# Inverse of the first delta rule on 32x32 diagonal blocks, with its running value kept in PSUM

## The chip, the core and the metric

The kernel runs on one core of a Trainium2 chip. The core has a matrix engine (TensorE, here PE, its weight loads PEld), three engines for elementwise work (VectorE or DVE, ScalarE or ACT, GpSimd or POOL), a queue that starts DMA transfers (SyncE, SP), an on-chip memory of 128 partitions, and PSUM, eight banks of 512 f32 per partition that PE writes. The engines run their own instruction lists and wait for each other with semaphores. The metric is device time in microseconds of one execution, median of several.

## The reference, cut to what matters

Two transformer layers over 256 tokens of width 2048. The second layer has two recurrences side by side. The first (16 heads of 64, "rwkv7") is

```
Sa = einsum('bhvk,bhk->bhv', S, a_t)
S  = S * w_t + Sa * b_t + v_t * k_t ;  y_t = S r_t
```

The kernel does it by chunks of 64 tokens: 4 chunks x 16 heads = 64 pairs. For each pair it needs the inverse of a unit triangular 64x64 matrix I - N, with N made of products of a and b of the chunk. Two pairs lie above each other in the 128 partitions (chunk c in partitions 64c to 64c+63), so a tile "of 32 units" [128, 32, 64] holds all of them; unit 16 cp + x is head x of chunk pair cp. The second recurrence (gated delta rule, 8 heads of 128) has its own inverse, which stands behind the first recurrence and is not changed. It needs decay matrices exp(F_i - F_j), masked to one triangle, for 8 heads and two halves of the tokens (tiles gd_x and gd_aqk_t).

## The kernel before, in words

Most of the kernel streams weights through PE in three products each (high and low parts). The change lies in the stretch between the input projection of the second layer and its output projection, where PE runs small f32 products. Every engine's list is written out by hand; an engine takes its instructions in that order, and a wait holds all that stand behind it.

**The inverse.** The products that fill N and the three other triangles (`gram_products`, groups i of the list GRAMS, banks from GRAM_BANKS) go through DVE (`gram_masks`), which multiplies by masks, writes nt_r, akt, rbt and rkt, and puts the 1x1 level under the diagonal of x_r and of xt_r with predicated copies. Then five levels k = 0 to 4 double the size of the inverted blocks. A level has, for each quarter b of the units (8 units), `inverse_z` (PE: N times X, 64x64 products), a mask of level k+1 on DVE into z_r, `inverse_x` (PE: X transposed times Z), an addition into x_r on DVE, and `inverse_turn`, the transpose of x_r into xt_r on DVE. The last level writes xt_r alone. Quarters of one level are interleaved on PE and DVE. Between them stand `value_products` (z1, copied by ACT), `decay_rows` (PE spreads the sums of the second recurrence's gates to PSUM, from which ACT makes both decay tiles with Relu and Exp) and the key grams of the second recurrence (L1227).

**Behind it.** Four groups make wt (L1239, copied by ACT at L1796) and the inverted values in banks 4 to 7 (L1164 again). On DVE `gd_lower` (L2600) multiplies the key grams into gd_x and `gd_begin` (L2641, L2643) cuts out its chunks.

**The recurrence.** Four turns g: PE multiplies the state into the values (L1255), DVE and ACT copy a half each into rw_u (L2657, L1802), PE makes the state products (L1270, L1276, L1283) and outputs (L1290, L1291), DVE updates the state (L2667, L2668). In turns 2 and 3 PE also transposes gd_x (L1265). DVE multiplies the sigmoid of z into proj2 in turn 1 (L2660), ACT makes this sigmoid in turn 0 (L1804). The query products (L1324) follow, then the second inverse.

POOL masks the decay tiles with affine_select (L643) and makes the first state (L637). SP starts the first two weight loads of the output projection when the recurrence's outputs are made.

Of the kernel before, what the change touches and what calls it, by code (L numbers as in the profile page):

```python
# [12 lines left out]
ALU = mybir.AluOpType  # L13
# [3 lines left out]
P = 128  # L17
# [52 lines left out]
def build(nc, a, out):  # L70
    ctx = ExitStack()
    with ctx:
# [171 lines left out]
        x_r = slot("rw_x", HO + 8 * KB, UNITS)  # L244
        GRAMS = [(cp, kind, g) for cp in range(2) for kind, g in (("b", 0), ("b", 1), ("x", 0), ("k", 0), ("k", 1))]
        GRAM_BANKS = (0, 2, 4, 6, 0, 2, 4, 6, 2, 6)
        xt_r, z_r = slot("rw_xt", R0, UNITS), slot("rw_z", R1, UNITS)
# [3 lines left out]
        gn_sq = slot("gn_squares", R5)  # L251
# [18 lines left out]
        z_sig = slot("gd_z_sig", R1)  # L270
# [12 lines left out]
        def bcc(m, n):  # L283
            return m.unsqueeze(1).to_broadcast([P, n, 64])


# [7 lines left out]
                "e_prev", "kk_root", "e_plus", "e_minus", "gd_sig_qk", "gd_sq", "gd_l2_root", "gd_sig_v", "gate_kept", "at_kept"],  # L294
            "vector": ["wf_spread", "f_raw", "rnn_out", "rows_rounded", "x_rescaled", "lora_lo", "ab_out", "lora_out", "lora_in", "kk", "r_shifted", "gd_cum",
                "gd_tok_out", "l_prev", "gd_scalars", "kk_mean", "kk_rows", "rk", "kk_out", "at_made", "rw_bonus", "gd_cv_qk", "rt_made",
                "gd_silu_qk", "bt_made", "gd_cv_v", "gd_l2_mean", "kw_made", "gd_silu_v", "l2_rows", "gd_qk"],
# [142 lines left out]
        def _(sp):  # L440
# [106 lines left out]
        def _(gp):  # L547
# [85 lines left out]
            for x in (x_r, xt_r):  # L633
                last = gp.tensor_copy(x[:], bcc(chunk_eye, 32))
            last.then_inc(step("eyes_made"), 1)
            gp.wait_ge(S("rw_gram"), 20)
            gp.memset(state[:], 0.0).then_inc(S("rw_state"), 1)  # L637
            for half in range(2):
                hs = slice(4 * half, 4 * half + 4)
                for o, g, base, cm in ((0, x_g, -1, 1), (1, aqk, 0, -1)):  # L640
                    v = g[:].rearrange("p (c h) n -> p c h n", c=2)[:, :, hs, :]
                    gp.wait_ge(S("gd_gam"), 2 * half + o + 1)
# [15 lines left out]
        def _(pe):  # L658
# [477 lines left out]
            def gram_products(i):  # L1136
# [6 lines left out]
                l = {"b": bt_f, "k": Kw, "x": None}[kind]  # L1143
                for n in range(4 * g, 4 * g + 4) if l is not None else range(8):
                    for c in range(2):
                        tc = slice((2 * cp + c) * CH, (2 * cp + c + 1) * CH)
                        for half in range(2):
                            r = slice(64 * half, 64 * half + 64)
                            o = bank(GRAM_BANKS[i] + half)[64 * c:64 * c + 64, :]
                            if l is None:  # L1150
                                last = mm(o[:, n * 64:(n + 1) * 64], at_f[r, n, tc], bt_f[r, n, tc], start=(n == 0), stop=True,
                                          skip_group_check=True)
                            else:
                                last = mm(o[:, (n % 4) * P:(n % 4 + 1) * P].rearrange("p (m t) -> p m t", m=2), l[r, n, tc],
                                          AR[r, :, n, tc], start=(n % 4 == 0), stop=True, skip_group_check=True)
# [12 lines left out]
            def value_products(cp):  # L1168
                if cp:
                    pe.wait_ge(S("rw_z1_out"), 1)  # L1170
                pe.wait_ge(S("rw_gram_out"), 20)
                for b in range(2):
                    last = of_chunks(bank(2 + b), lambda r, u: akt[r, u, :], lambda r, u: v_tok2[r, u // 16, hc(u % 16)], 8,
# [3 lines left out]
            def inverse_z(k, b):  # L1177
                pe.wait_ge(S("inv_x_out"), 4 * k + b + 1)
                wait(pe, S("inv_z_out"), 4 * k + b - 1)
                of_chunks(bank(b % 2), lambda r, u: nt_r[r, u, :], lambda r, u: x_r[r, u, :], 8, 8 * b).then_inc(S("inv_z"), 1)  # L1180

            def inverse_x(k, b):
                pe.wait_ge(S("inv_z_out"), 4 * k + b + 1)
                if k == 0:
                    pe.wait_ge(S("rw_gram_out"), 20 if b >= 2 else 14)
                else:
                    pe.wait_ge(S("inv_xt_out"), 4 * k - 4 + b + 1)
                x_lhs, x_rhs = (xt_r, z_r) if k < 4 else (z_r, xt_r)
                of_chunks(bank(4 + b), lambda r, u: x_lhs[r, u, :], lambda r, u: x_rhs[r, u, :], 8, 8 * b).then_inc(S("inv_x"), 1)

            def decay_rows(half):
                pe.wait_ge(S("gd_fall"), 2 * half)
                over_heads(2, row_sums[:], 4 * half, 4 * half + 4,
                           sel_r[0:2 * H, :].bitcast(F32)).then_inc(step(f"gd_g_rows{half}"), 1)

            for i in range(8):
                gram_products(i)
            for k in range(5):
                if k == 0:
                    pe.wait_ge(S("rw_gram_out"), 10)  # L1200
                inverse_z(k, 0)
                if k == 0:
                    gram_products(8)
                inverse_z(k, 1)
                if k == 0:
                    gram_products(9)
                inverse_x(k, 0)
                inverse_z(k, 2)
                inverse_x(k, 1)
                if k == 0:  # L1210
                    value_products(0)
# [1610 lines left out]
```

## Time and profile before

| | us |
|---|---|
| device time, median of 3 runs | 2889.12 (2886.62 to 2892.81) |
| span of the profiled execution | 2882.8 |
| PE busy in it | 2851.3 (99%) |
| DVE busy | 1590.1 (55%) |
| ACT busy | 1164.0 (40%) |
| POOL busy | 70.5 (2%) |

The span is from the first to the last instruction of the profiled execution; the device time is measured around the whole launch. In the view of 40 slices each digit is a tenth. A record is one instruction as the profiler saw it: each f32 product of the small stages leaves two weight loads and two matmuls. In the lists of time, a row merges neighbouring records of one kind: the first number is the start, the second the time from the first start to the last end, xN their count. "128*128" or "64*64" is rows times columns of the array that a matmul uses.

### The profile page before, as it was taken

To read this page: it belongs to the slowest core of one execution; us is meant where nothing else is said; L and a number is where in the kernel's file an instruction comes from. 1 tells how busy PE (TensorE), PEld (TensorE's weight loads), DVE (VectorE), ACT (ScalarE), POOL (GpSimd) and SP (SyncE) were. 2 spreads that over 40 slices of the span, in tenths; PEclk is the share of its full clock that TensorE was granted. 3 is DMA by queue.
4 is the path that set the end of the run, shared out by engine and by line. 5 is a ranking of instruction groups with operands and counts; after the bars stand their busy time and mean duration, and the time that the engine had idled before them with its cause. 6 is when DMAs were issued, how large, how long until landed. Compare 5 with 4: busy or idle time off the path is not lost.

```text
span 2882.8 us, 41255 instructions
## 1 busy us (share of the span) xinstructions
PE 2851.3 (99%) x17984; PEld 2456.9 (85%) x17984; DVE 1590.1 (55%) x1321; ACT 1164.0 (40%) x952; POOL 70.5 (2%) x130
## 2 busy tenths in 40 slices
PE   8999999999999999999999999999999999999998
PEld 8999888888888888888889999998788888888887
DVE  5757554544555554454447667876664545454445
ACT  4345443333443333333335443433444333333333
POOL 0000000000000000002002000010000000000000
PEclk9999999999999999999999999999999999999999
DMA  6555556666555555555556544400355555555554
GB/s 223 165 162 186 163 161 190 190 194 192 184 189 190 189 189 189 189 189 190 191 195 220 171 136 159 149 3 33 111 181 190 189 190 189 189 189 189 190 194 170
DMA packets 257441, 501.09 MB, mean 174 GB/s; under 512 B 12288, under 2 KB 17739, under 8 KB 256923
## 3 DMA queue, kind: packets, MB, share of 16 engines
q1 hardware_dynamic: 257307, 499.06, 53.4%
q8 instruction: 113, 1.85, 0.3%
q14 instruction: 21, 0.17, 0.0%
HBM read 496.74 MB, written 2.10 MB: 173 GB/s over the span
## 4 chain that ended last, share of the span: by engine, by line
PE 96%; DVE 3%; ACT 0%; issue 0%; DMA 0%; SPq 0%; DVEq 0%; ACTq 0%
PE psum L724 23%; PE psum L726 23%; PE psum L725 23%; PE psum L709 5%; PE psum L712 5%; PE psum L711 5%; PE psum L1164 2%; DVE weight_lo L1934 1%; PE psum L775 1%; PE psum L1039 0%; PE psum L663 0%; PE psum L1024 0%; PE psum L890 0%; PE psum L910 0%; PE psum L900 0%; DVE rw_gram L2566 0%
## 5 line engine op out<-in xcount | busy, mean ns | idle before, releaser
L1934 DVE TENSOR_TENSOR weight_lo<-weight_raw,weight_hi 128x2048 fp32r<-128x2048 f32 x460 | 1054.2, 2292 | 1088.7 <-ACT weight_hi L1470 1088.1
L1470 ACT ACTIVATE weight_hi<-weight_raw 128x2048 fp32r<-128x2048 f32 x460 | 881.6, 1916 | 1495.8 <-PE psum L726 1210.0
L724 PE MATMUL psum<-weight_hi,h_both 128*128 128x512 f32 x1856 | 724.9, 391 | 0.0
L726 PE MATMUL psum<-weight_hi,h_both 128*128 128x512 f32 x1856 | 722.5, 389 | 0.0
L725 PE MATMUL psum<-weight_lo,h_both 128*128 128x512 f32 x1856 | 722.1, 389 | 0.0
L726 PEld LDWEIGHTS psum<-weight_hi,h_both 128*128 128x128 f32 x1856 | 348.4, 188 | 72.8
L725 PEld LDWEIGHTS psum<-weight_lo,h_both 128*128 128x128 f32 x1856 | 348.6, 188 | 71.3
L724 PEld LDWEIGHTS psum<-weight_hi,h_both 128*128 128x128 f32 x1856 | 348.5, 188 | 71.3
L709 PE MATMUL psum<-h_both,weight_hi 128*128 128x256 f32 x1408 | 401.6, 285 | 6.8 <-DVE weight_lo L1934 6.7
L711 PE MATMUL psum<-h_both,weight_lo 128*128 128x256 f32 x1408 | 398.4, 283 | 0.0
L712 PE MATMUL psum<-h_both,weight_hi 128*128 128x256 f32 x1408 | 398.3, 283 | 0.0
L709 PEld LDWEIGHTS psum<-h_both,weight_hi 128*128 128x128 f32 x1408 | 270.0, 192 | 11.7 <-DVE weight_lo L1934 5.8
L711 PEld LDWEIGHTS psum<-h_both,weight_lo 128*128 128x128 f32 x1408 | 270.1, 192 | 0.1
L712 PEld LDWEIGHTS psum<-h_both,weight_hi 128*128 128x128 f32 x1408 | 270.1, 192 | 0.0
L724 PE MATMUL psum<-weight_hi,ffn_hi 128*128 128x512 f32 x672 | 261.9, 390 | 0.0
L726 PE MATMUL psum<-weight_hi,ffn_lo 128*128 128x512 f32 x672 | 261.5, 389 | 0.0
L725 PE MATMUL psum<-weight_lo,ffn_hi 128*128 128x512 f32 x672 | 261.4, 389 | 0.0
L724 PEld LDWEIGHTS psum<-weight_hi,ffn_hi 128*128 128x128 f32 x672 | 126.1, 188 | 26.5 <-issue 0.6
L726 PEld LDWEIGHTS psum<-weight_hi,ffn_lo 128*128 128x128 f32 x672 | 126.1, 188 | 26.2
L725 PEld LDWEIGHTS psum<-weight_lo,ffn_hi 128*128 128x128 f32 x672 | 126.1, 188 | 26.1
L726 PE MATMUL psum<-weight_hi,y_lo 128*128 128x512 f32 x320 | 125.2, 391 | 0.0
L724 PE MATMUL psum<-weight_hi,mixed_hi 128*128 128x512 f32 x256 | 101.5, 396 | 3.3 <-DVE y_lo L2771 3.3
(526 smaller groups left out, 2184.1 us busy)
## 6 DMA issues: line engine op xcount, KB each, us to landing
weight_raw<-in_w_in SPq DMA_DIRECT2D x144, 1024.0 KB, 5.4
weight_raw<-in_w_ffn_in SPq DMA_DIRECT2D x88, 1024.0 KB, 5.0
weight_raw<-in_w_ffn_out SPq DMA_DIRECT2D x44, 1024.0 KB, 5.1
weight_raw<-in_ffn_w_gate SPq DMA_DIRECT2D x44, 1024.0 KB, 5.1
weight_raw<-in_ffn_w_up SPq DMA_DIRECT2D x44, 1024.0 KB, 5.2
weight_raw<-in_ffn_w_down SPq DMA_DIRECT2D x44, 1024.0 KB, 5.1
weight_raw<-in_w_out SPq DMA_DIRECT2D x32, 1024.0 KB, 5.2
weight_raw<-in_w_branch_rnn SPq DMA_DIRECT2D x8, 1024.0 KB, 5.1
```

Of the source, the lines that this page charges most:

```text
L709: mm(acc[:, f, :], wh[:, k, c], xh, start=(start and k == 0 and f % 2 == 0), stop=False, skip_group_check=True)
L711: mm(acc[:, f, :], wl[:, k, c], xh, start=False, stop=False, skip_group_check=True)
L712: last = mm(acc[:, f, :], wh[:, k, c], xl, start=False, stop=(stop and k == CK - 1), skip_group_check=True)
L724: mm(acc[:, t, :], xh[:, c], wh[:, k, :], start=(start and k == 0), stop=False, skip_group_check=True)
L725: mm(acc[:, t, :], xh[:, c], wl[:, k, :], start=False, stop=False, skip_group_check=True)
L726: last = mm(acc[:, t, :], xl[:, c], wh[:, k, :], start=False, stop=(stop and k == CK - 1), skip_group_check=True)
L775: last = tr(pair(2)[:, k, t * P:(t + 1) * P], act_up[:, t, k * P:(k + 1) * P], ident[:])
L1164: last = mm(o[r, u * 64:(u + 1) * 64], lhs(r, u0 + u), rhs(r, u0 + u), start=(u == 0), stop=True, skip_group_check=True)
L1470: A(hi[j % g.hi][:], raw[j % g.ring][:], ACT.Copy).then_inc(hi_ready, 1)
L1934: V.tensor_tensor(lo[r][:], raw[r][:], hi[j % g.hi][:].bitcast(F32), ALU.subtract).then_inc(lo_ready, 1)
```

## The change

The inverse now works on the two 32x32 blocks on the diagonal of each 64x64 matrix. They are kept in compact tiles of 32 columns (x_c, xt_c, z_c: [128, 32, 32]), four blocks above each other in the partitions. Levels k = 0 to 3 run on halves cp of 16 units, and each product is a 32x32 one at partitions 32q (`block_products`). The value of X is kept in PSUM (bank cp): an identity product puts the first X there (`inverse_begin`), each level's product adds to it, and ACT copies it to x_c (`block_copy`), from where DVE turns it. The last level, the lower corner of each 64x64 matrix, is two products of 32x32 blocks (`corner_z`, `corner_x`, with an identity product in front of the second) and copies into the two column halves of xt_r. The gram groups come in another order with other banks; the x grams are only made for the diagonal blocks; the predicated copies into xt_r are gone.

The decay differences are made by two engines: ACT makes gd_x with Relu (`decay_falls`), DVE makes gd_aqk_t with subtract and min (`decay_rises`), each starting at another bank. The four Exp come at the end, and the masks of gd_x before those of gd_aqk_t. DVE copies wt in place of ACT (`key_states`). The inverted values of the second chunk pair move into turn 2 of the recurrence; gd_lower and gd_begin move into turns 0 and 1, the silu of z to the end of turn 2, its sigmoid to turn 2. POOL builds masks of 32 columns (block_masks, upper_rows). SP's second weight load waits for gn_var too, since gn_squares and rw_z now share memory with its ring slot.

The core of the diff:

```diff
+        x_c, xt_c, z_c = slot("rw_x", HO + 8 * KB, BLOCKS), slot("rw_xt_blocks", HO + 12 * KB, BLOCKS), slot("rw_z", R1, BLOCKS)
...
+        GRAMS = [(cp, kind, g) for cp in range(2) for kind, g in (("b", 0), ("b", 1), ("x", 0))] + \
+                [(cp, "k", g) for cp in range(2) for g in range(2)]
+        GRAM_BANKS = (0, 2, 4, 6, 4, 6, 4, 6, 4, 6)
...
             for j, src in enumerate(wo2.sources(0)):
+                if j == 1:
+                    sp.wait_ge(*at_step("gn_var"))
...
+            def block_products(b, lhs, rhs, cp, start):
+                for u in range(16 * cp, 16 * cp + 16):
+                    for q in range(4):
+                        r = slice(32 * q, 32 * q + 32)
+                        last = mm(bank(b)[r, (u % 16) * 32:(u % 16 + 1) * 32], lhs(r, u, q % 2), rhs(r, u), start=(start and u % 16 == 0),
+                                  stop=True, skip_group_check=True)
+                return last
+            def inverse_begin(cp):
+                pe.wait_ge(S("rw_gram_out"), 6 + 6 * cp)
+                pe.wait_ge(*at_step(f"turned{cp}"))
+                mm(bank(cp), ident[:], x_c[:, quarter(cp), :].rearrange("p u n -> p (u n)"), start=True, stop=False,
+                   skip_group_check=True)
+            def inverse_z(k, cp):
+                if k:
+                    pe.wait_ge(*at_step(f"x_out{k - 1}{cp}"))
+                block_products(2 + cp, lambda r, u, b: nt_r[r, u, 32 * b:32 * b + 32], lambda r, u: x_c[r, u, :], cp,
+                               True).then_inc(step(f"inv_z{k}{cp}"), 1)
+            def inverse_x(k, cp):
+                pe.wait_ge(*at_step(f"z_out{k}{cp}"))
+                pe.wait_ge(*at_step(f"turned{k - 1 if k else ''}{cp}"))
+                block_products(cp, lambda r, u, b: xt_c[r, u, :], lambda r, u: z_c[r, u, :], cp, False).then_inc(step(f"inv_x{k}{cp}"), 1)
+            def corner_z(cp):
+                pe.wait_ge(*at_step(f"x_out3{cp}"))
+                for u in range(16 * cp, 16 * cp + 16):
+                    for c in range(2):
+                        r = slice(64 * c, 64 * c + 32)
+                        last = mm(bank(2 + cp)[64 * c + 32:64 * c + 64, (u % 16) * 32:(u % 16 + 1) * 32], nt_r[r, u, 32:64], x_c[r, u, :],
+                                  start=(u % 16 == 0), stop=True, skip_group_check=True)
+                last.then_inc(step(f"inv_z4{cp}"), 1)
+            def corner_x(cp):
+                pe.wait_ge(*at_step(f"turned3{cp}"))
+                pe.wait_ge(*at_step(f"z_out4{cp}"))
+                mm(bank(2 + cp), ident[:], xt_c[:, quarter(cp), :].rearrange("p u n -> p (u n)"), start=True, stop=True,
+                   skip_group_check=True)
...
+            for i in range(4):
+                gram_products(i)
+            inverse_begin(0)
+            inverse_z(0, 0)
+            gram_products(4)
+            inverse_x(0, 0)
+            gram_products(5)
+            inverse_z(1, 0)
+            gram_products(6)
+            inverse_begin(1)
+            inverse_z(0, 1)
+            inverse_x(1, 0)
+            gram_products(7)
...
+            inverse_z(3, 0)
+            value_products(0)
+            inverse_z(2, 1)
+            inverse_x(3, 0)
+            value_products(1)
+            inverse_x(2, 1)
+            corner_z(0)
+            decay_rows(0)
+            inverse_z(3, 1)
+            corner_x(0)
+            inverse_x(3, 1)
+            corner_z(1)
+            decay_rows(1)
+            corner_x(1)
+            key_states(0)
+            inverted_values(0)
+            key_states(1)
+            key_products()
...
+                if g == 2:
+                    inverted_values(1)
+                    pe.wait_ge(S("rw_uv"), 2)
...
+            def block_copy(k, cp):
+                act.wait_ge(*at_step(f"inv_x{k}{cp}"))
+                A(x_c[:, quarter(cp), :], blocks_of(cp), ACT.Copy).then_inc(step(f"x_out{k}{cp}"), 1)
...
+            def inverse_turn(k, cp):
+                dve.wait_ge(*at_step(f"x_out{k}{cp}"))
+                V.transpose(xt_c[:, quarter(cp), :], x_c[:, quarter(cp), :]).then_inc(step(f"turned{k}{cp}"), 1)
...
+            def decay_rises(half):
+                dve.wait_ge(*at_step(f"gd_g_rows{half}"))
+                for b in (1, 0):
+                    if b == 0:
+                        dve.wait_ge(S("gd_fall"), 2 * half + 1)
...
+                if g == 2:
+                    dve.wait_ge(S("gd_z_sig"), 1)
+                    V.tensor_tensor(proj2[:, 40:48, :], proj2[:, 40:48, :], z_sig[:], ALU.mult).then_inc(S("gd_z_silu"), 1)
+                if g < 2:
+                    gd_lower(g, 0, 8)
+                    dve.wait_ge(S("gd_n"), g + 1)
+                    gd_begin(x_gc, x_g, low_c[0], g).then_inc(S("gd_x_out"), 1)
```

## Rows read from the trace of the kernel before

**Rows 1.** The page: span, busy time of PE, granted clock by 40 slices.

```profile
span 2882.8 us, 41255 instructions
PE 2851.3 (99%) x17984; PEld 2456.9 (85%) x17984; DVE 1590.1 (55%) x1321; ACT 1164.0 (40%) x952; POOL 70.5 (2%) x130
...
PEclk9999999999999999999999999999999999999999
```

**Rows 2.** Windows of the stage: us, busy time (records) of five engines, clock, DMA.

```profile
1894.45:1903.28 8.83, 8.29 (x322) 7.19 (x321) 7.33 (x15) 1.02 (x1) 0.00 (x0) 1.00 0.03 6
1903.28:1955.50 52.22, 50.16 (x1503) 48.50 (x1504) 41.41 (x72) 15.73 (x39) 4.80 (x5) 1.00 0.01 3
1955.50:1963.79 8.29, 7.82 (x267) 7.42 (x263) 8.16 (x21) 2.17 (x4) 0.00 (x0) 1.00 0.02 6
1963.79:1987.42 23.63, 23.47 (x721) 22.72 (x721) 10.81 (x14) 10.98 (x16) 0.00 (x0) 1.00 0.01 3
```

**Rows 3.** Chain that ended last, pieces in the inverse: start, us, what.

```profile
1909.63 14.14 PE psum L1164 x480
1923.77 1.92 PE psum L1045 x8
...
1935.37 10.66 PE psum L1164 x352
...
1957.24 0.60 DVE rw_xt L2586
```

**Rows 4.** Waits, 1894.5 to 1987.4: total us, times, longest.

```profile
DVE rw_z L2579 <- PE psum L1164: 10.2, 8, 2.4
```

**Rows 5.** List by time, PE, small products: start, us, line, tile, operands, count.

```profile
1957.88 2.08 PE L1164 MATMUL psum<-rw_z,rw_xt 64*64 64x64 f32 x64 [0.42 <-DVE rw_xt L2586]
...
1896.25 1.11 PE L1151 MATMUL psum<-proj,a_tilde_r 64*64 64x64 f32 x64
...
1896.25 0.24 PE L1151 MATMUL psum<-proj,a_tilde_r 64*64 64x64 f32 x4
...
1718.37 0.36 PE L1063 MATMUL psum<-ident,gdn_b 16*128 16x8 f32 x2
1718.60 0.36 PE L1064 MATMUL psum<-ident,gdn_small 16*128 16x8 f32 x2
```

**Rows 6.** The same list: one-tile products and what follows them.

```profile
1945.96 2.05 PE L1227 MATMUL psum<-proj 128*128 128x128 f32 x16
1947.94 0.27 PE L1164 MATMUL psum<-rw_x,rw_gram 64*64 64x64 f32 x2
...
1991.41 3.64 PE L1039 MATMUL psum<-gn_squares,head_cols 128*32 128x256 f32 x16
1994.98 0.33 PE L1164 MATMUL psum<-gd_z_chunks,gd_xt_chunks 64*64 64x64 f32 x4
```

**Rows 7.** Groups by line, 1883 to 2037: busy us, mean ns, idle before, releaser.

```profile
L2579 DVE TENSOR_TENSOR rw_z<-psum,chunk_masks 128x512 f32<-128x512 f32 x20 | 13.6, 680 | 10.4 <-PE psum L1164 10.2 <-DVE rw_x L2551 0.3
...
L1812 ACT ACTIVATE gn_squares<-psum 128x512 f32<-128x512 f32 x4 | 2.4, 592 | 0.0
```

**Rows 8.** List by time, DVE: gd_lower and gd_begin before the recurrence.

```profile
1957.74 2.16 DVE L2600 SCALAR_TENSOR_TENSOR gd_x<-psum,gdn_token_scalars,gd_x 128x128 f32<-128x128 f32 x8
...
1959.93 1.39 DVE L2641 TENSOR_TENSOR gd_x_chunks<-gd_x,chunk_masks 64x512 f32<-64x512 f32 x2
...
1961.35 0.69 DVE L2643 TENSOR_TENSOR gd_x_chunks<-gd_x_chunks,chunk_masks 128x512 f32<-128x512 f32 x1
```

**Rows 9.** DMA queue of instructions and busy time, 1890 to 1990.

```profile
q8 instruction: 23, 0.38, 1.7%
...
1890.00:1990.00 100.00, 96.76 (x2878) 92.62 (x2877) 70.65 (x122) 32.95 (x64) 8.78 (x8) 1.00 0.03 7
```

**Rows 10.** Windows around the one fall of the clock near the stage.

```profile
2068.50:2074.01 5.51, 2.25 (x13) 1.57 (x13) 4.91 (x5) 4.03 (x3) 0.00 (x0) 1.00 0.58 182
2074.00:2080.00 6.00, 5.99 (x19) 4.80 (x20) 3.29 (x2) 0.00 (x0) 0.00 (x0) 0.72 0.02 9
```

More of the change, by code:

```diff
@@ new lines, in corner_x @@
+            def corner_x(cp):
[3 more added lines that the diff above has]
+                   skip_group_check=True)
+                for u in range(16 * cp, 16 * cp + 16):
+                    for c in range(2):
+                        r = slice(64 * c + 32, 64 * c + 64)
+                        last = mm(bank(2 + cp)[64 * c:64 * c + 32, (u % 16) * 32:(u % 16 + 1) * 32], z_c[r, u, :], xt_c[r, u, :],
+                                  start=(u % 16 == 0), stop=True, skip_group_check=True)
+                last.then_inc(step(f"inv_x4{cp}"), 1)
@@ new lines, in decay_rows, with key_products @@
+            def decay_rows(half):
+                if half:
+                    pe.wait_ge(S("gd_fall"), 2)
+                    pe.wait_ge(S("gd_rise"), 2)
+                else:
+                    pe.wait_ge(S("rw_z1_out"), 1)
+                over_heads(4, row_sums[:], 4 * half, 4 * half + 4,
+                           sel_r[0:2 * H, :].bitcast(F32)).then_inc(step(f"gd_g_rows{half}"), 1)
+            def key_products():
+                pe.wait_ge(S("gd_fall"), 4)
+                pe.wait_ge(S("gd_rise"), 4)
+                for c in range(2):
+                    tk = slice(c * P, (c + 1) * P)
+                    for h in range(4):
+                        last = mm(bank(4 + c)[:, h * P:(h + 1) * P], cv[:, 4 + h, tk], cv[:, 4 + h, tk], start=(h == 0), stop=True,
+                                  skip_group_check=True)
+                last.then_inc(step("gd_gram"), 1)
@@ L1236, in _, with key_states @@
+            def key_states(cp):
+                pe.wait_ge(*at_step(f"xt_left{cp}"))
+                pe.wait_ge(*at_step(f"xt_right{cp}"))
+                if cp == 0:
+                    pe.wait_ge(*at_step("x_out31"))
+                    pe.wait_ge(*at_step("turned31"))
+                for n in range(8):
+                    for half in range(2):
                         for c in range(2):
-                            x = 8 * (b % 2) + n
+                            x = 8 * half + n
                             tp = slice(64 * c, 64 * c + 64)
@@ L1260, in _ @@
                 if g >= 2:
+                    pe.wait_ge(S("gd_n"), g - 1)
                     if g == 3:
@@ new lines, in _ @@
+            for k, cp in ((0, 0), (1, 0), (0, 1), (2, 0), (1, 1)):
+                block_copy(k, cp)
+            values_copy(0)
+            block_copy(3, 0)
+            values_copy(1)
+            block_copy(2, 1)
+            decay_falls(0)
+            block_copy(3, 1)
+            decay_falls(1)
+            for o, g in ((0, x_g), (1, aqk)):
+                for half in range(2):
+                    act.wait_ge(S("gd_rise" if o else "gd_fall"), 2 * half + 2)
+                    v = g[:].rearrange("p (c h) n -> p c h n", c=2)[:, :, 4 * half:4 * half + 4, :]
+                    A(v, v, ACT.Exp, scale=1.0 if o else -1.0).then_inc(S("gd_gam"), 1)
@@ L1838, in _ @@
             scaled_k(1)
-            act.wait_ge(*at_step("gn_var"))
+            act.wait_ge(S("gd_z_silu"), 1)
             chunk_hi(1)
@@ L2593, in gd_lower, with key_states @@
+            def key_states(cp):
+                dve.wait_ge(S("rw_wt"), cp + 1)
+                for g in (2 * cp, 2 * cp + 1):
+                    last = V.tensor_copy(wt[:, :, g * CH:(g + 1) * CH], bank(g).rearrange("p (n t) -> p n t", n=NT))
+                last.then_inc(S("rw_wt_out"), 1)
             def gd_lower(c, h0, h1):
@@ L2648, in chunk_turn @@
                 V.transpose(xt_gc[:, u, :], x_gc[:, u, :]).then_inc(S("gd_xt_out"), 1)
-            dve.wait_ge(S("gd_n"), 2)
-            for b in range(2):
-                gd_begin(x_gc, x_g, low_c[0], b).then_inc(S("gd_x_out"), 1)
             for g in range(4):
```

289 lines of the change are left out of this document (126 added, 163 removed), and 2 rows, old and new, of the table STEPS.

## The prediction

> **What bounds the kernel now.** The page comes first: PE is busy 99% of the span and its clock is full in nearly every slice [rows 1]. But the change touches one stage only, so I cut the span at that stage with the windows view. From 1894.45 us (first gram product) to 1987.42 us (query products, the first work that the change leaves alone) are 92.97 us; PE is busy 89.7 of them, DVE 67.7, ACT 29.9 [rows 2]. The reader should see that DVE is nearly full only in the first window (7.33 of 8.83) and in the third (8.16 of 8.29), and PE in all four. The chain of waits says the same: long unbroken pieces of the 64x64 products at L1164, between them the spread rows at L1045, while DVE enters it only before 1909 and around 1955 [rows 3]. The view of waits has DVE waiting 10.2 us for L1164 [rows 4]. So in the inverse PE's instruction stream sets the end, and what changes there goes to the total one for one: nothing behind it hangs on absolute time, because each later weight load is released by steps of this chain.
>
> **The unit of price.** Each f32 product leaves two records on PE. 64 records of 64x64 tiles last 2.08 us from first start to last end, one record 0.22, so 63 gaps share 1.86 us: 29.5 ns a record where two tiles of the array take turns [rows 5]. The x-gram products use four tiles: (1.11-0.22)/63 = 14.1 ns [rows 5]. Both are some 58 ns for one tile. 256 columns on one tile take 3.57/16 = 223 ns a record [rows 6], and loading 128 weight columns against 8 moving ones takes 112 ns (two records each 0.225 us) [rows 5]. So a tile costs about 0.87 ns for each column, moving or weight, whichever is more, and a 32x32 product keeps its tile for about 30 ns. The new products walk over four diagonal tiles: 30/4 = 7.5 ns. Four x-gram records start inside 0.24-0.22 = 0.02 us, 7 ns apart [rows 5]; that is the closest that PE is seen to issue in a run of four. I take 8 ns. The trace has nothing that lasts at such a rate: 14.1 ns is the fastest over 64 records. Ends: 6.5 ns and 14.1 ns.
>
> **The change part by part (PE).** A. Removed: twenty z and twenty x groups of 32 records, 29.2 ns each in my sum (the 29.5 above holds small waits), 40 x 0.93 = 37.4 us. B. Added: 4 levels x 2 halves x 2 = 16 block products of 128 records, 16 x 1.02 = 16.4 us. C. Corner products, 4 groups of 64 records on only two tiles, 30/2 = 16 ns: 4.1 us (2.0 at 8 ns, 7.5 at 29.2). D. Four identity products of 512 columns, two records each, 2 x 0.446 from L1039 [rows 6]: 3.6 us. E. x grams: 256 records of 8 ns for 128 of 14.6: +0.2. F. key_states alternates halves and so uses four tiles where L1239 used two: 128 records at 14.6 for 29.2, -1.9. Grams, value products, decay rows, key grams and inverted values keep number and price; inverted_values(1) only moves to the third turn of the recurrence, where PE is serial too. Sum: 37.4 - 16.4 - 4.1 - 3.6 - 0.2 + 1.9 = 15.0 us less work.
>
> G. Changes of tile shape. The 16 turns L1227 start at 1945.96 and the next product at 1947.94 [rows 6]: 1.98 us for 16 x 0.112 = 1.79, so about 0.17 us for coming back. Before, the stage has 10 changes of shape; afterwards I count 35 in the written order (32x32, 64x32, 64x64, 128x128, and 16 rows). 25 x 0.17 = +4.3 us. Whether 64x64 to 32x32 costs what 128x128 to 64x64 does no row shows: ends 0.05 and 0.4, that is +1.3 and +10.
>
> H. Waits. 92.97 less work at these prices (85.0) less ten changes (1.7) leaves 6.3 us of waiting before. For afterwards I walked the new orders of PE, DVE and ACT with 0.69 us for each 128x512 step on DVE and 0.59 on ACT [rows 7] and 0.2 behind the last product. A level of one half costs 1.2 + 0.7 + 1.2 + 0.6 = 3.7 us, and the four products of a level with their grams need over 4 us of PE, so the two halves hide each other. Four holes remain: 1.2 us before the first product (PE waits for masks and the turn of half 0), 0.9 at the second corner, and two of 2.0 us in the recurrence. Those come from moved DVE work: gd_lower and gd_begin now stand behind the state update of turns 0 and 1. Eight steps at L2600 are 2.16 us, gd_begin 1.39 + 0.69 [rows 8]: 4.3 us in which the copy of u queues, while PE needs it 0.95 us later than it could be made (3 x 0.93 of other products, less 0.93 + 0.22 + 0.69). In the first it meets PE at the u product (2.0 us); in the second inverted_values(1) waits for gd_n (2.0). Sum 6.1: -0.2 us. The moved silu product (2.29 us) stands before the last copy of u, behind transposes and state products of PE: nothing. ACT's decay work halves on the Relus, and the rest is split with DVE: off the path. SP's second weight load now waits for gn_var, which PE makes at the start of the second inverse, long before the weight is split: nothing. DVE is no bound: its early masks lose the eight copies into xt_r, and I count some 32 us of work for it in the 53 us up to the recurrence, where it had 57 in 69.
>
> **Total.** -15.0 + 4.3 - 0.2 = -10.9 us; the walk with the same prices, after the same walk over the old order came out 0.4 us under its measured 92.97, gives -10.4. I take -10.5. The profiled span is 2882.8 us, 6.3 under the median 2889.1; what lies around the span doesn't change, so 2872.3 of span, 2878.6 us of device time.
>
> **A rule against the row.** The four-tile row issues a record each 14.1 ns over 64 records. The Trainium skill (TensorE: Matmul & The Clock Gate, Back-to-back issue gap) gives 1 to 64 columns about 60 cycles each, a floor of some 25 ns between starts. By that floor for each record whatever its tile, the 2048 block records alone would take 51 us, more than all forty removed products, and this would be slower. The row contradicts it as a floor of the whole array, but agrees with it as one of a tile. The same page (Terms and Specs) says that the queue holds 64 instructions, half of those that the row's 64 records and their weight loads make, so a slower supply might hide in it.
>
> **Rivals.** 1. Supply of instructions binds (slower side). Twice the records cover the same products; if PE can be fed a record and its weight load only every s ns over long stretches, price B grows. By the walk the total moves 2.1 us for each ns; it is level at s = 13, +4.3 us at 14.6, +18 at 20, +31 at 25 (2920 us). For it: nothing faster than 14.1 ns lasts beyond 64 records; 16 KB of instructions come in one packet per about 250 records and loads (23 packets for 5755 in 100 us) and take 1.7% x 16 x 100 / 23 = 1.2 us each [rows 9], as long as one block product: fetched one by one they allow 9.2 ns, +2.5 us on my sum. Against: 7 ns in the burst. Faster than 14.1 I hold for likely, slower than 16 for one case in seven.
>
> 2. Little difference. s between 10.5 and 15.5, or 8 ns with changes of shape at 0.4 us (-3): 2883.3 to 2894.9.
>
> 3. The clock falls. It fell once near this stage, after 5.5 us in which PE was busy 2.25: 0.72 granted in the next 6 us [rows 10]. If the many short waits did this in the inverse, 26 us of small products would go at 1.2 GHz, up to +26, 2904 us. Against: the longest hole I find is 2 us, and the old stage with its waits stayed at 1.00 [rows 2].
>
> 4. Better than forecast: 6.5 ns, shape changes near 0.05 us: -14 and another -4, 2871 us.
>
> **Chances.** Forecast with its neighbourhood down to rival 4 (2870 to 2883.3): 0.65. Rival 2: 0.17. Rival 1 beyond 15.5 ns: 0.14. Rival 3: 0.04. 0.2%, about what a measurement of this kernel can tell from no change, is 5.8 us: faster 0.65, same 0.17, slower 0.18. The range takes in rival 4 and the supply up to about 16.5 ns, +9: 2871 to 2898; some 0.15 lies above it, a few hundredths below.
>
> **What would show it.** Block products (L1164's successor) as groups of 128 records some 1.0 us apart, 8 ns a record: right. 14 ns or more: step B is wrong. Gaps marked "issue" of 0.17 us at changes of shape: G. A PE hole of 2 us ended by the copy of u after the first state update, and one ended by gd_lower: H. Recurrence starting near 1948 where it did at 1963.8, query products near 1977. It would also be wrong if DVE or ACT ended most of PE's waits inside the levels, or if granted clock under 1.00 appeared between 1894 and 1977.

## The result, and the profile after

The changed kernel takes 2925.85 us (median of 4 runs, 2924.66 to 2928.60) where the kernel before takes 2889.39 (4 runs, 2886.62 to 2892.81): a ratio of 1.0129 with a 95% interval of 1.0115 to 1.0143, 36.5 us slower. I had forecast 10.5 us faster, with a range that ended at 2898.

The profiled execution of after has a span of 2926.9 us, 44.1 more than before's. The stage, from the first gram product to the query products, holds most of that. The windows view of after, cut as [rows 2] is (columns: stretch, length, busy time and records of PE, PE's weight loads, DVE, ACT and POOL, granted clock, DMA share, GB/s):

```profile
1901.69:1905.50 3.81, 2.91 (x160) 2.64 (x160) 2.48 (x4) 1.02 (x1) 0.00 (x0) 1.00 0.02 6
1905.50:1992.72 87.22, 61.77 (x2810) 50.90 (x2809) 28.83 (x55) 12.81 (x28) 0.53 (x1) 0.72 0.02 4
1992.72:1999.96 7.24, 7.24 (x213) 7.05 (x209) 3.27 (x5) 3.77 (x4) 4.24 (x4) 0.79 0.02 5
1999.96:2031.51 31.55, 28.14 (x786) 27.01 (x785) 18.70 (x35) 10.88 (x16) 0.00 (x0) 0.89 0.01 3
sum 129.82, PE 100.06 PEld 87.60 DVE 53.28 ACT 28.49 POOL 4.77; mean PE 25.02 PEld 21.90 DVE 13.32 ACT 7.12 POOL 1.19
```

The stage lasts 129.82 us in place of 92.97: +36.85, which is the measured loss. Three things are new. PE is busy only 61.77 of 87.22 us in the inverse, though DVE (28.83) and ACT (12.81) are idle most of it. The window holds 2810 records in 87.22 us, 31.0 ns each, while the same kernel before ran its 1503 in 52.22. And the granted clock is 0.72 where it was 1.00: much of the stage runs at the 1.2 GHz level. The other 7 us of the profiled span lie ahead of the stage, in one stretch at the lower level that this execution has and before's has not. Of the variants below whose code ahead of the stage is the same, e2, e3 and e4 lack it (1.00 in the same window) and e6 has it (0.63), so it belongs to single executions and is no part of the result:

```profile
1702.00:1716.00 14.00, 14.00 (x40) 8.75 (x40) 4.43 (x1) 2.06 (x4) 0.00 (x0) 0.51 0.00 1
```

Where PE is idle is told by its waits in the stage (who waited for what, total us, times, longest):

```profile
PE psum L1207 <- issue: 16.8, 9, 2.5
PE psum L1233 <- issue: 3.8, 2, 2.0
PE psum L1171 <- issue: 2.9, 2, 1.9
PE psum L1370 <- DVE rw_u L2770: 1.8, 1, 1.8
PE psum L1192 <- DVE gd_x L2713: 1.4, 1, 1.4
...
PE psum L1214 <- DVE rw_xt_blocks L2668: 0.7, 1, 0.7
```

Here "issue" is idle time in which the profile shows nothing that the engine waited for. L1207 is the line of the block products, L1233 that of the corner z products, L1171 that of the x grams. Nearly everything is "issue": no other engine is waited for. The list by time shows where in a group the idle time falls (start, length, what, count, idle time before it):

```profile
1903.60 1.01 PE L1171 MATMUL psum<-proj,a_tilde_r 64*32 64x32 f32 x95
1905.56 0.40 PE L1171 MATMUL psum<-proj,a_tilde_r 64*32 64x32 f32 x33 [0.96 <-issue]
...
1908.74 1.62 PE L1207 MATMUL psum<-rw_x,rw_gram 32*32 32x32 f32 x128
...
1911.33 0.44 PE L1207 MATMUL psum<-rw_z,rw_xt_blocks 32*32 32x32 f32 x28
1913.61 1.45 PE L1207 MATMUL psum<-rw_z,rw_xt_blocks 32*32 32x32 f32 x100 [1.84 <-issue]
1914.99 0.45 PE L1171 MATMUL psum<-proj,a_tilde_r 64*32 64x32 f32 x28
1917.36 1.25 PE L1171 MATMUL psum<-proj,a_tilde_r 64*32 64x32 f32 x100 [1.91 <-issue]
1918.53 0.64 PE L1207 MATMUL psum<-rw_x,rw_gram 32*32 32x32 f32 x28
1921.10 1.59 PE L1207 MATMUL psum<-rw_x,rw_gram 32*32 32x32 f32 x100 [1.93 <-issue]
```

The stall cuts groups of 128 into 28 and 100. A dependence would stand between groups; this one comes after every 128 records (100 + 28), whatever they are, and PE resumes at 1913.61, 1917.36 and 1921.10, 3.75 us apart. 128 records with their weight loads are 256 instructions, and the DMA view of the long window has for the queue of instructions (packets, MB, share):

```profile
q8 instruction: 22, 0.36, 1.7%
```

22 packets of 16 KB for 2810 records: one packet for 128 records. Each took 1.7% x 16 x 87.22 / 22 = 1.1 us, but one came only each 87.22 / 22 = 4.0 us. This is rival 1's shape, and step B's price at 8 ns a record is where the forecast broke. That is still an inference from one trace.

### The profile page after: what moved, and what is told of

Read it like the earlier page. It is cut to its first block, busy times and chain, and to the rows that moved or that the text cites. A ratio compares the mean times of both kernels' runs of the same rounds, so it can differ in the third digit from the quotient of the medians.

```text
span 2926.9 us, 43521 instructions
## 1 busy us (share of the span) xinstructions
PE 2868.8 (98%) x19144; PEld 2463.4 (84%) x19144; DVE 1575.3 (54%) x1301; ACT 1162.5 (40%) x940; POOL 68.8 (2%) x134
## 4 chain that ended last, share of the span: by engine, by line
PE 95%; DVE 3%; issue 1%; ACT 0%; DMA 0%; SPq 0%; DVEq 0%; ACTq 0%
PE psum L746 23%; PE psum L748 23%; PE psum L747 23%; PE psum L731 5%; PE psum L734 5%; PE psum L733 5%; PE psum L1192 1%; PE psum L1207 1%; DVE weight_lo L2031 1%; PE psum L797 1%; PE psum L1061 0%; PE psum L685 0%; PE psum L1182 0%; PE psum L1067 0%; PE psum L1046 0%
## 5 line engine op out<-in xcount | busy, mean ns | idle before, releaser
L746 PEld LDWEIGHTS psum<-weight_hi,ffn_hi 128*128 128x128 f32 x672 | 126.2, 188 | 26.7 <-issue 0.6
L747 PEld LDWEIGHTS psum<-weight_lo,ffn_hi 128*128 128x128 f32 x672 | 126.2, 188 | 26.2
```

Source lines behind the costliest of these rows:

```text
L746: mm(acc[:, t, :], xh[:, c], wh[:, k, :], start=(start and k == 0), stop=False, skip_group_check=True)
L747: mm(acc[:, t, :], xh[:, c], wl[:, k, :], start=False, stop=False, skip_group_check=True)
```

## Experiments

Theory S (supply): PE gets its instructions in pieces of 128 records and their loads, one in about 3.75 us, 29 ns a record, whatever they compute. Rival T: the price is in the array, in quick turns among four tiles. Rival C: the loss is one of clock. Rival D: it comes from the decay half of the change or the moved DVE steps. The first four kernels ran on the same chip beside 8 runs of the kernel before (2889.16 us).

**e1_streams.** A kernel that computes nothing of the reference: streams of 1024 records, wide products between them.

> A kernel of its own that computes nothing of the reference: after some wide products it issues streams of small products, each stream 1024 records on PE (f32 products leave two records each; the bf16 stream 1024 too), with 16 wide products between streams. Theory S (supply): PE gets its instructions in pieces of 16 KB, 128 records with their weight loads, and one piece takes some 3.75 us, so no long stream goes below 29.3 ns a record: 64x64 on two tiles 29-30, 64x64 on four tiles 29-30, 32x32 on four tiles 29-30, 32x32 with 8 moving columns 29-30, bf16 29-30, with stalls of about 2 us at each 128 records where the tiles are faster. Theory T (tile price, as predicted): 29.2, 14.6, 8, 7, and bf16 near 6.5; one tile 30. The clock alone would give about double T with no stalls. The stream inside a hardware loop (a body of 128 records, 8 times) says whether a repeated body is supplied faster; S expects the same 29 unless the body stays in the core.

Its list by time, first two-tile 64x64 products, then 32x32 on four tiles, 32x32 in bf16, and the hardware loop:

```profile
26.96 30.08 PE L62 MATMUL psum<-right,left 64*64 64x64 f32 x1024
...
111.20 2.34 PE L77 MATMUL psum<-right,left 32*32 32x32 f32 x255
115.59 1.27 PE L77 MATMUL psum<-right,left 32*32 32x32 f32 x128 [2.05 <-issue]
119.32 1.93 PE L77 MATMUL psum<-right,left 32*32 32x32 f32 x128 [2.46 <-issue]
...
269.96 1.19 PE L97 MATMUL psum<-right_h,left_h 32*32 32x32 bf16 x128 [2.29 <-issue]
...
307.83 11.12 PE L105 MATMUL psum<-right,left 32*32 32x32 f32 x1024
```

Two tiles: 29.3 ns a record, without a stall. The 32x32 stream begins with 255 records in 2.34 us, (2.34 - 0.22) / 254 = 8.3 ns, then stalls after each 128; 1024 records take 26.7 us. With 64x64 on four tiles they took 26.4, with 8 moving columns 26.6, in bf16 26.2. Among these streams, which the tiles could run faster, the time doesn't depend on the work, so S holds and T falls. A piece lasts 3.45 to 3.73 us in most rows here, 27 to 29 ns a record. The last row decides: the same 32x32 instructions as a loop of 128 records, run 8 times, take 11.12 us, 1.40 for each turn. The windows (32x32 straight, looped, then 64x64 on four tiles and 32x32 on one tile alone, both straight):

```profile
111.20:137.80 26.60, 13.36 (x1025) 12.46 (x1024) 0.00 (x0) 0.00 (x0) 0.63 0.02 4
307.80:318.90 11.10, 10.27 (x1025) 9.40 (x1024) 0.00 (x0) 0.00 (x0) 1.00 0.00 0
...
71.00:97.00 26.00, 16.33 (x1015) 15.37 (x1019) 0.00 (x0) 0.00 (x0) 1.00 0.02 5
...
197.30:250.00 52.70, 52.70 (x1024) 52.70 (x1024) 0.00 (x0) 0.00 (x0) 0.52 0.01 2
```

In the loop nothing is fetched (0 GB/s against 4) and PE is never starved: 10.9 ns a record with the jumps back, 8.3 in the straight stream's first burst. Stalls and clock don't go together one for one. Straight 32x32 code had 0.63, but the 64x64 stream on four tiles stalled for 1.4 to 1.6 us in each piece as well, kept 1.00 and took the same 26 us, so the low clock isn't what sets this time. The one-tile stream never stalled and ran at 0.52: 69 records in its first 2 us at full clock, 29 ns each, then 52.9 ns each at the lower level (567 in 30 us). Both theories had 29 to 30 for it and no fall of the clock.

**e2_half_blocks.** In the kernel after:

```
-                    for q in range(4):
+                    for q in range(2):
```

> The changed kernel with the block products of the lower two partition quarters left out (1024 of 2048 block records; the second chunk of each pair isn't inverted). Theory S: 1024 records x 29.3 ns = 30 us less than the changed kernel's 2925.9, so 2893 to 2899. Theory T with my 8 ns: 8 us less, 2918. If the halved clock were the whole cause: about 16 ns a record, 2909.

Measured: 2900.11 us (5 runs), ratio 1.0055 (1.0031 to 1.0078), 1.1 us above S's range. 1024 records less are 25.7 us less than after, 25.1 ns each (in the traces the stage is 23.0 us shorter, 22.5 ns each), nearest to S; the array's own 9 ns would have given 9 us. The clock's 2909 lies inside the interval, which reaches 2912, so this run alone doesn't rule rival C out. Of the stalls at L1207 3.2 us are left.

**e3_fill_stalls.** Two wide identity products stand before each group of z products:

```
+                for _ in range(2):
+                    mm(bank(2 + cp), ident[:], x_c[:, quarter(cp), :].rearrange("p u n -> p (u n)"), start=True, stop=True,
+                       skip_group_check=True)
```

> The changed kernel with two wide identity products (512 columns, f32, 0.446 us a record at full clock, 4 records) ahead of each z product, 16 in all, 14.3 us of PE work but only 32 records; their result is overwritten. Theory S: they run while the next piece of instructions comes, so the time stays within -6 to +4 us of 2925.9, and the granted clock of the stage rises from 0.72; what it falls below 2925.9 is the clock's part. If PE's work set the end, +14 us or more (2940).

Measured: 2933.78 us (4 runs), ratio 1.0158 (1.0140 to 1.0175), 8 us over after: outside both theories' ranges. The traces tell where. These are the windows of after and of e3 from the end of the first stall inside a block group to the end of the stage's last stall; 415 records of the stage stand ahead of each:

```profile
1913.61:1984.39 70.78, 48.09 (x2428) 41.55 (x2428) 20.89 (x37) 9.11 (x18) 0.53 (x1) 0.71 0.02 4
...
1908.09:1981.18 73.09, 55.37 (x2429) 39.15 (x2428) 19.95 (x36) 8.51 (x17) 0.53 (x1) 0.87 0.02 4
```

As many records take nearly as long, 29.2 and 30.1 ns each, with seven of the eight pairs of wide products among them, 12.5 us of work for 2.3 us more. The granted clock rose from 0.71 to 0.87 and nothing came back for it. That is S, and it speaks against rival C. The rest stands outside: 0.6 us ahead of the first stall, and 4.2 behind the last (51.28 for 47.12 us), where 32 more of the kernel's own records are left and the clock is 0.75 in place of 0.82. Why the clock is lower there isn't shown.

**e4_gd_in_slots.** gd_lower of turns 0 and 1 stands between the copy of u and the state update, where DVE waits for PE, and not behind the update:

```
                 V.tensor_copy(u_tok[tp, 0:512], bank(6 - 2 * cp)[tp, :]).then_inc(S("rw_u"), 1)
+                if g < 2:
+                    gd_lower(g, 0, 8)
```

> The changed kernel with gd_lower put between the copy of u and the state update of turns 0 and 1, where DVE waits for PE, and gd_begin left behind the state update. The two holes of PE in the recurrence (1.8 and 1.4 us in the trace of after) go: -3 us, 2922.5 to 2925; if the pieces of instructions set the end there as well, nothing.

Measured: 2919.52 us (4 runs), ratio 1.0104 (1.0087 to 1.0121): 6.3 us under after, twice what was expected; the two intervals overlap, so the traces have to say it. The recurrence, from its first product to the query products, in e4 (after's is the fourth window of the stage above):

```profile
1994.26:2020.40 26.14, 25.58 (x786) 24.66 (x785) 18.53 (x35) 10.87 (x16) 0.00 (x0) 1.00 0.02 4
```

The same 786 records take 5.4 us less (31.55 to 26.14). Of the two holes of step H, 1.8 and 1.4 us, 0.3 are left. The rest goes with the clock, 1.00 where it was 0.89. The 64 products behind the second hole (L1192) took 3.68 us at the lower level in after and take 2.08 here.

**e6_decay_one_engine.** ACT makes the decay differences alone again:

```
+                    for o, g in ((0, x_g), (1, aqk)):
...
+                                last = A(g[:, 8 * c + h, :], rows_h, ACT.Relu, bias=col_h, scale=-1.0 if o else 1.0)
...
-            decay_rises(0)
...
-            decay_rises(1)
```

> The changed kernel with its decay differences all on ACT again (16 more ACT steps of about 0.3 us, 16 DVE steps fewer), nothing else different. Supply theory: the loss of 36.5 us lies in PE's small products alone, so this half of the change is worth within -1 to +3 us of the kernel after (2925 to 2929; ACT has room, but its last copy of x waits 2.4 us longer behind eight more steps). If the shared decay were part of the loss, this would be 5 us or more faster (under 2921).

Measured: 2925.47 us (4 runs), ratio 1.0129 (1.0108 to 1.0149) to the kernel before of its session (2885.61): no difference to after's 1.0129, though the interval is some 6 us wide to either side. The stage in its trace takes 130.44 us, 0.6 more than after's. This half of the change is worth about nothing either way, and what of rival D it covers falls; what the moved DVE steps cost is e4's 5.4 us in the stage.

**e5_loop_bodies.** If a loop's body isn't fetched again, up to which size?

> A kernel by itself that leaves the whole computation out: loops whose bodies are 32x32 products on four tiles, 256 records x 4, 384 x 4, 512 x 4, 640 x 4 and 1024 x 3 iterations (L62), then eight loops of 32 records x 4, then 512 products with 64 weight columns and 32 moving ones on two tiles (L95, 1024 records); wide products between. In e1_streams a body of 128 records ran 8 times in 11.12 us, while straight code took 26.7 us for as many. If a loop's body stays with the engine up to a size, the bodies under it run at about 8.5 ns a record (256 x 4 in 9 to 12 us: about 4 more for the first pass, 5.3 to 7.4 ns) and those above it at the straight rate of 26 to 29 ns a record (512 x 4: 53 to 60 us). From the first bursts of e1_streams (159 to 255 records) I put the limit between 256 and 512 records. If instead every jump back fetched the body anew, 256 x 4 would take 27 to 30 us too. The eight short loops: 1024 records; 0.3 us for each jump back, 32 x 0.27 + 32 x 0.3 = 18 us. Last stream: if records are what is fed, 26 to 30 us as for every other stream of 1024; if 64 weight columns keep a tile 58 ns, the same 29.3 ns: no difference.

The loops of 256 x 4, of 640 x 4 and (its first rows) of 1024 x 3 records:

```profile
27.34 1.80 PE L62 MATMUL psum<-right,left 32*32 32x32 f32 x190
31.28 0.76 PE L62 MATMUL psum<-right,left 32*32 32x32 f32 x66 [2.14 <-issue]
32.20 7.29 PE L62 MATMUL psum<-right,left 32*32 32x32 f32 x768 [0.16 <-issue]
...
140.38 1.93 PE L62 MATMUL psum<-right,left 32*32 32x32 f32 x128 [1.53 <-issue]
143.84 19.45 PE L62 MATMUL psum<-right,left 32*32 32x32 f32 x1958 [1.52 <-issue]
...
203.41 1.18 PE L62 MATMUL psum<-right,left 32*32 32x32 f32 x72 [2.07 <-issue]
209.09 0.97 PE L62 MATMUL psum<-right,left 32*32 32x32 f32 x56 [4.50 <-issue]
212.36 1.93 PE L62 MATMUL psum<-right,left 32*32 32x32 f32 x128 [2.30 <-issue]
```

The first pass is starved, the three others of the 256 body take 7.29 us for 768 records, 9.5 ns. The limit that I had put between 256 and 512 is higher: bodies of 384, 512 and 640 records stay too (640: from the fourth stall on 1958 records, 38 of them of the first pass, in 19.45 us, 9.9 ns). 1024 don't: every pass is fetched anew, with 4.50 and 4.07 us idle at the two jumps back. Eight short loops of 32 x 4 took 17 us against 18 expected; 64 weight columns with 32 moving ones took 30.05 us, as expected no cheaper.

**e7_levels_in_loop and e8_levels_straight.** The decisive pair. All four levels of the inverse use the same addresses, so they can be the turns of one loop. In e4's kernel the grams go ahead, the rest behind, and the levels become

```
                with pe.Fori(0, 4) as k:
                    for cp in range(2):
                        at_level(f"x_out0{cp}", k, 2, cp)
                        block_products(2 + cp, lambda r, u, b: nt_r[r, u, 32 * b:32 * b + 32], lambda r, u: x_c[r, u, :], cp,
                                       True).then_inc(done, 1)
                    for cp in range(2):
                        at_level(f"z_out1{cp}", k, 4, cp)
                        block_products(cp, lambda r, u, b: xt_c[r, u, :], lambda r, u: z_c[r, u, :], cp, False).then_inc(done, 1)
```

where at_level is a wait carried by a small product into a free bank. e8 has `for k in range(4)` in place of the first line and nothing else different.

> e4's kernel (2919.5 us) with the four levels of the inverse as one loop of TensorE: its body is the two z and the two x products of a level (512 records) and four small products that carry the waits (8 records), run four times; all gram products stand before it, and value, corner and decay products after. In e5_loop_bodies a body of 640 records stayed with the engine: the first pass at 28 ns a record, the next three at 9 to 10. Supply theory: 3 x 512 records x (28.5 - 9) = -30 us, four small products a level and the loop's jumps +3, and a few us more or less for the new order of the rest: 2887 to 2898 us. If the loss came from the work, the shape changes or the waits between the engines, the loop gives nothing: within 5 us of the straight form, e8_levels_straight.

> The same kernel as e7_levels_in_loop, the same instructions in the same order, written out four times in place of the loop. Supply theory: 520 records a level x 28.5 ns = 14.8 us a level, as in the kernel after: 2918 to 2928 us, and 25 to 32 us more than e7_levels_in_loop.

Measured beside 8 runs of the kernel before (2888.23): e7 2898.94 us (5 runs), ratio 1.0037 (1.0023 to 1.0051); e8 2923.09 us (4 runs), ratio 1.0121 (1.0104 to 1.0138). e7 is 0.9 us above its range and e8 inside its own; the same instructions in the same order are 24.15 us faster as a loop, 0.9 less than the least expected. The windows of the first level and of the other three, e7 and then e8:

```profile
1910.90:1923.60 12.70, 8.41 (x524) 7.55 (x520) 4.49 (x7) 0.60 (x1) 0.53 (x1) 0.73 0.02 5
1923.60:1945.30 21.70, 21.21 (x1560) 19.98 (x1560) 8.42 (x12) 3.58 (x6) 0.00 (x0) 0.85 0.00 0
```

```profile
1910.90:1924.10 13.20, 9.27 (x525) 8.43 (x521) 4.48 (x7) 0.60 (x1) 0.53 (x1) 0.67 0.02 5
1924.10:1968.90 44.80, 31.71 (x1559) 29.18 (x1555) 8.42 (x12) 3.58 (x6) 0.00 (x0) 0.50 0.02 4
```

The first level is alike. The other three take 21.70 us in the loop, with nothing fetched and PE busy 98%; straight they take 44.80, 28.7 ns a record. The difference, 23.1 us, is nearly all of the measured one. DVE and ACT did the same work in both, and the shapes change as often, so waits and shape changes can't be the cause: S is shown in the kernel itself. The slowdown of the clock (0.85 against 0.50) goes along with it.

**e9_loop_no_carriers.** The carriers give way to a counter that PE clears itself, and the second spread of decay rows no longer waits:

```
-                    pe.wait_ge(sem_, k * stride + (n - stride))
-                    mm(bank(2 + cp)[:, 0:32], ident[:], ident[:, 0:32], start=True, stop=True, skip_group_check=True)
+                    pe.wait_ge(S(name), 1)
+                    pe.sem_clear(S(name))
```

> e7_levels_in_loop (2898.9 us) with two edits. The four small products a level that carry the loop's waits are gone (each held PE for about 0.31 us from its start to the next block product, 16 of them: -5.0); a counter that TensorE clears itself, raised once for each z and each copy of x, takes their place (0 to +0.1 us each: up to +1.6). And the second spread of decay rows no longer waits 1.9 us for the differences of the first, which now come before the corner copies (-1.9), and the half-clock stretch behind that hole (3.78 and 3.32 us for groups of 2.0 and 2.1 at full clock) goes with it (-3.0). Sum -8.3 to -9.9: 2889.0 to 2890.6, range 2885 to 2895. Supply theory: the first pass of the loop stays at 12 to 13 us, the next three come down from 6.5 to about 5 us. It would be level with the kernel before (2888.6) within 0.2%.

Measured: 2886.35 us (11 runs) beside 2887.97 (15 runs), ratio 0.9996 (0.9987 to 1.0005): level, inside the range expected, though 12.6 us came off e7 (measured on another chip; in the stages of the two traces 11.4) where my sum had at most 9.9. The stage, from the first gram product at 1896.72 to the query products at 1987.29, takes 90.57 us (before 92.97). The levels after the first:

```profile
1930.47 2.42 PE L1207 MATMUL psum<-rw_x,rw_gram 32*32 32x32 f32 x256 [0.23 <-ACTq L1853]
1932.76 2.42 PE L1207 MATMUL psum<-rw_z,rw_xt_blocks 32*32 32x32 f32 x256
1935.41 2.43 PE L1207 MATMUL psum<-rw_x,rw_gram 32*32 32x32 f32 x256 [0.23 <-ACTq L1853]
```

256 records start 2.29 us ahead of the next 256, 8.9 ns each: my 8 ns was a fair price for an instruction that is there.

**e10_corners_by_masks.** From e9 the corners' identity products (4 records) are taken out, and DVE places the lower blocks:

```
-                mm(bank(2 + cp), ident[:], xt_c[:, quarter(cp), :].rearrange("p u n -> p (u n)"), start=True, stop=True,
-                   skip_group_check=True)
...
+                V.tensor_scalar(xt_r[:, quarter(cp), 32:64], xt_c[:, quarter(cp), :], lower_rows[:], None, ALU.mult)
```

> e9_loop_no_carriers (2886.35 us) without the identity products of the corners: DVE takes the lower blocks from the transposed tile itself (one more masked step of 0.48 us and one more copy of 0.69 us for each half of the tokens). PE saves two products of 1.06 us and four changes of shape of some 0.1 to 0.17: -2.1 to -2.8 us, if DVE stays off the path: before key_states PE waits for the right blocks of both halves, which come 0.69 us later each, up to +0.7. So 2883.5 to 2885.0 us, 0.1% under the kernel before or up to 0.2%. It tells no theories apart; it asks whether the layout of 32x32 blocks, freed of its supply, can come out under the kernel before.

Measured: 2889.86 us (11 runs) beside 2887.47 (15 runs), ratio 1.0006 (0.9997 to 1.0015): 3.5 us over e9, a miss on the other side of no change. The two ran on different chips and their intervals overlap, but the traces agree: the stage takes 94.31 us for 90.57. Its list by time behind the corners, and the same places in e9:

```profile
1947.55 2.21 PE L1253 MATMUL psum<-rw_xt_blocks,rw_z 32*32 32x32 f32 x128
1951.35 1.99 PE L1287 MATMUL psum<-rw_xt,a_tokens 64*64 64x64 f32 x64 [1.59 <-DVE rw_xt L2685]
1953.27 3.77 PE L1070 MATMUL psum<-row_sums,head_rows_r 16*128 16x256 f32 x8
```

```profile
1952.69 1.16 PE L1286 MATMUL psum<-rw_xt,a_tokens 64*64 64x64 f32 x64
1953.79 1.99 PE L1067 MATMUL psum<-row_sums,head_rows_r 16*128 16x256 f32 x8
```

The products taken out had covered DVE's copies. The saved 2.2 us came back as a wait of 1.59 us, and behind the wait the clock fell: the decay rows took 3.77 us for 1.99. I had priced the wait at up to 0.7 us and the clock at nothing.

## Why the prediction was wrong, point by point

- **What bounds the kernel: half right.** PE's stream does set the end of the stage in both kernels. But "PE is busy" had hidden that its stream has two limits: 29 ns a record for 64x64 on two tiles is the tiles' price, and it happens to be the supply's as well (e1: 29.3 ns without a stall). Before stood close to the edge at which supply begins to bind.
- **The unit of price: right, and used for the wrong thing.** 0.87 ns a column gave 7.5 ns and I took 8. While instructions are there, the x gram in after runs 95 records in 1.01 us, (1.01 - 0.22) / 94 = 8.4 ns, e9's loop 8.9. I wrote that nothing lasts at such a rate, and still took the burst's rate for the stream's.
- **Step B is the one that failed.** 16 block products at 1.02 us were to take 16.4; straight code feeds a record each 27 to 29.3 ns, so their 2048 records take 55 to 60 us. In a loop, with only the first level fetched, the four levels took 12.70 + 21.70 us with carriers.
- **Rival 1 was this mechanism, and its chance was too low.** Its slope of 2.1 us per ns from -10.5 at 8 ns gives +29 at 27 and +34 at 29.3. Its own points don't lie on that slope: from +18 at 20 ns to +31 at 25 are 2.6 us per ns, which gives +36 and +42. Measured +36.5. What kept its price small was listed in its favour: 1.2 us for a packet of about 250 instructions, "fetched one by one they allow 9.2 ns" with 128 records in it. The packet does take 1.1 us; the queue's next one comes 3.45 to 4 us after it. I took the time of a transfer for the time between transfers; the before trace had no stretch in which PE ran dry, so it couldn't show the latter. [Rows 9] count 23 packets in 100 us, 4.3 us apart, a rate near the one that turned out to be the limit.
- **The rule against the row.** The Trainium skill (TensorE: Matmul & The Clock Gate, Back-to-back issue gap) has a floor of some 60 cycles, 25 ns, between starts for 1 to 64 columns. As a floor for the whole array the runs contradict it: 9.5 ns across four tiles over 768 records (e5). As a number it would have come near, +31 us by rival 1's point at 25 ns, for another reason: the supply in straight code, 27 to 29 ns.
- **C, F: right in price, swallowed in after.** The 64 corner records on two tiles in e9 take 1.20 us, (1.20 - 0.22) / 63 = 15.6 ns (16 forecast); key_states 1.16, 14.9 ns (14.6). In after the corners wait 3.8 us for supply, and key_states runs at the lower clock.
- **D, G: right or too high.** The identity product with its change of shape takes 1.06 us. That leaves 0.17 us for the change, as forecast. Changes between 128x128 and 32x32 tiles are cheaper: in e7 a carrier's two records take 0.34 us to the next start where the loads are 0.22, and a block group before a carrier 1.22 against 2.29 / 2 in e9, so 0.12 and 0.08 us.
- **H: right in place, near in size.** 0.7 us before the first product (1.2 forecast), the second corner 0.7 (0.9), the two holes of the recurrence 1.8 and 1.4 (2.0 each), ended by the copy of u and by gd_lower as told. What they cost was more than their length (e4: 5.4 us in the trace, 6.3 in device time).
- **Rival 3 came true as a consequence.** I had argued from holes of at most 2 us. Here they came every 3.75 us over the whole inverse. The groups outside it show the price: 128 records of value products had a mean of 297 ns where a record lasts 218 at full clock (L1192), and the decay rows 5.8 us in sum where both spreads take 4.0 in e9. Once the levels were fed, the clock came back some 2 us later in e9 and 7 us later in e7. But stalls alone don't bring it down (e1's 64x64 stream on four tiles), and what in PE's work does isn't shown. How many of the 36.5 us are clock I can't separate: a starved stream loses little by it, its wide neighbours do.
- **The total.** What lies around the span isn't 6.3 us: after's profiled execution took 2928.60 us for a span of 2926.9, 1.7 more. Most of the 6.3 was one execution of before that was faster than the median. The forecast of -10.5 doesn't hang on it.
- **The decay half** had been put at no cost: right (e6).

Open are what sets the distance between packets, whether anything but loops shortens it, and what lowers the clock.

## What to carry to other kernels

Count PE's instructions as well as its columns: in straight code budget about 28 ns for each record with its weight load (f32 and bf16 alike in e1), and 3.5 to 4 us for each 128 of them, and cut tiles finer only if that budget stays under the array's time or if the code repeats with the same addresses, so that it can be a loop of up to 640 records. When a rate in a trace is faster than anything that lasts in it, it may show a buffer and not a stream. And before taking PE work out, ask which copy it covers; a bare wait costs its length and, as in e10, sometimes the clock behind it.

## What the runs showed of the hardware

- PE's instructions come in 16 KB pieces of 256. A piece is 1.1 us on the queue, but pieces follow each other only every 3.45 to 4.0 us, alone on the chip (e1) and in the full kernel alike. 157 to 255 records run ahead of the first stall where the tiles are fast (e1, e5).
- A loop's body of up to 640 records is not fetched again; one of 1024 is. A turn of the 128-record loop took 1.40 us; a jump back in e5, e7 and e9 left PE idle 0.15 to 0.25 us.
- Fed, four diagonal tiles of 32x32 take an f32 record each 8.4 to 9.5 ns, and 1.9 us in place of 1.3 for 128 at the lower clock (e1); one tile alone takes 29 ns at full clock and 52.9 at the lower one.
- Stalls and granted clock are two things: with a stall of 1.4 to 1.6 us in each piece the 64x64 stream on four tiles kept 1.00, and without any stall the one-tile stream fell to 0.50 (e1). At a clock of 0.87 in place of 0.71 the starved inverse was no faster (e3).
- With the supply out of the way, the layout of 32x32 blocks is level with the 64x64 one in this kernel (e9: 0.9996); the first pass through the loop is still fetched there, and takes 12.5 us.
